# Writing a 64-expert loop out on all engines, moving the token lists behind gate-and-up, and dropping empty scatter entries

## The reference

```python
def moe(x, w_router, router_bias, w_gate_e, w_up_e, w_down_e, w_gate_s, w_up_s, w_down_s):
    t = x.reshape(-1, D_MODEL)
    ...
    def expert_step(acc, xs):
        wg, wu, wd, g = xs
        h = jax.nn.silu(t @ wg) * (t @ wu)
        return acc + (h @ wd) * g[:, None].astype(t.dtype), None
    routed, _ = lax.scan(expert_step, jnp.zeros_like(t), (w_gate_e, w_up_e, w_down_e, gates.T))
    shared = (jax.nn.silu(t @ w_gate_s) * (t @ w_up_s)) @ w_down_s
    return (routed + shared).reshape(shp)
```

## Time and profile before

| what | value |
|---|---|
| median of three runs | 1395.07 us |
| profiled execution, its own time: its span | 1394.2 us |
| PE busy | 1241.1 us (89%) |
| DVE busy | 777.2 us (56%) |
| ACT busy | 543.3 us (39%) |
| POOL busy | 407.7 us (29%) |
| DMA, mean over the span | 228 GB/s |
| loads of gate, up and down, each | 64 x 1024 KB |

### The profile page before, as it was taken

The page is one execution under the profiler, slowest core; times in us unless marked ns, Lnnn a source line. Parts: engine busy times, 40 slices in busy tenths (PEclk is TensorE's granted clock), DMA queues, the critical chain, the costliest instruction groups (busy, mean ns, idle before and its releaser), DMA issues.

```text
span 1394.2 us, 18458 instructions
## 1 busy us (share of the span) xinstructions
PE 1241.1 (89%) x6931; PEld 976.8 (70%) x6931; DVE 777.2 (56%) x1095; ACT 543.3 (39%) x722; POOL 407.7 (29%) x385
## 2 busy tenths in 40 slices
PE   6499978989999899969999999999999999999980
PEld 6499956789999897427666666666666666666650
DVE  2113589243311644537776666666666666666745
ACT  2231467242213312125444444444444444445522
POOL 2000234111100123251433343433444333433223
PEclk9699989599999997989999999999999999999995
DMA  9942020113223308327999999999999999999954
GB/s 191 286 151 81 16 86 2 68 38 100 76 91 115 126 1 343 147 83 276 365 361 350 343 345 343 346 340 342 351 347 342 344 334 341 342 343 342 356 106 152
DMA packets 92096, 317.49 MB, mean 228 GB/s; under 512 B 15586, under 2 KB 48516, under 8 KB 66804
## 3 DMA queue, kind: packets, MB, share of 16 engines
q1 hardware_dynamic: 65616, 257.03, 47.5%
q0 software_dynamic: 19280, 56.12, 20.5%
q10 hardware_dynamic: 7140, 3.50, 0.9%
HBM read 284.30 MB, written 47.97 MB: 238 GB/s over the span
## 4 chain that ended last, share of the span: by engine, by line
PE 77%; DVE 10%; issue 4%; DMA 3%; ACTq 2%; POOL 2%; ACT 2%; DVEq 0%; SPq 0%; POOLq 0%
PE bank L1925 26%; PE bank L1945 16%; PE bank L1661 9%; PE bank L1662 9%; PE bank L1820 4%; DVE onehot L1501 3%; PE bank L1888 3%; PE bank L1676 3%; ACTq L876 2%; PE bank L1850 2%; DVE L L1256 1%; DMA raw<-in_w_in_dram 1%; DVE mx L1262 1%; PE bank L1841 1%; PE bank L1867 1%
## 5 line engine op out<-in xcount | busy, mean ns | idle before, releaser
L1525 DVE TENSOR_TENSOR wgu_lo<-wgu,wgu_hi 128x4096 fp32r<-128x4096 f32 x64 | 282.5, 4414 | 2.7 <-ACT wgu_hi L1125 2.6
L788 POOL TENSOR_TENSOR spare<-spare 128x1 f32<-128x1 f32 x128 | 122.6, 958 | 445.7 <-DMA y_rows<-ysb,idx_u 406.1
L1945 PE MATMUL bank<-wd,hT 128*128 128x512 f32 x512 | 230.1, 592 | 0.9 <-DVE hT L1535 0.9
L1125 ACT ACTIVATE wgu_hi<-wgu 128x4096 fp32r<-128x4096 f32 x63 | 227.4, 3610 | 0.1
L1925 PE MATMUL bank<-wgu_hi,xgT 128*128 128x512 f32 x512 | 206.3, 403 | 2.6
L1925 PE MATMUL bank<-wgu_hi,xgT_lo 128*128 128x512 f32 x512 | 200.9, 392 | 0.0
L1925 PE MATMUL bank<-wgu_lo,xgT 128*128 128x512 f32 x512 | 200.6, 392 | 0.0
L1129 ACT ACTIVATE silu<-bank 128x256 f32<-128x256 f32 x64 | 24.5, 383 | 370.1 <-PE bank L1925 370.1
L1945 PEld LDWEIGHTS bank<-wd,hT 128*128 128x128 f32 x512 | 96.7, 189 | 98.0 <-issue 92.0
L1541 DVE COPY ysb<-bank 128x512 f32<-128x512 f32 x64 | 44.2, 691 | 162.5 <-PE bank L1945 162.5
L1925 PEld LDWEIGHTS bank<-wgu_hi,xgT 128*128 128x128 f32 x512 | 96.7, 189 | 23.4 <-issue 0.5
(11 more groups left out here) (287 smaller groups left out, 2391.6 us busy)
## 6 DMA issues: line engine op xcount, KB each, us to landing
wgu<-in_w_gate_e_dram SPq DMA_DIRECT2D x64, 1024.0 KB, 9.2
wgu<-in_w_up_e_dram SPq DMA_DIRECT2D x64, 1024.0 KB, 13.6
wd<-in_w_down_e_dram SPq DMA_DIRECT2D x64, 1024.0 KB, 7.8
raw<-in_w_in_dram SPq DMA_DIRECT2D x16, 1024.0 KB, 5.5
raw<-in_w_proj_a_dram SPq DMA_DIRECT2D x4, 1024.0 KB, 5.2
raw<-in_w_out_dram SPq DMA_DIRECT2D x4, 1024.0 KB, 5.2
bias_rows<-e_row POOLq DMA_DIRECT2D x1, 3072.0 KB, 34.6
x_lo_kept<-xT_lo SPq DMA_DIRECT2D x1, 2304.0 KB, 10.8
```

Of the source, the lines that this page charges most:

```text
L788: pool.tensor_tensor(spare[:, i:i + 1], spare[:, 0:1], spare[:, 0:1], ALU.mult).then_inc(s, 1)
L1125: act.activation(wgu_hi[u % 2][:], wgu[u % WSLOTS][:], ACT.Copy).then_inc(hi_by_act, 1)
L1525: v.tensor_tensor(wgu_lo[u % WSLOTS][:], w_[:], wgu_hi[u % 2][:].bitcast(F32), ALU.subtract).then_inc(lo_by_dve, 1)
L1945: last = mm(bank[3 + h][:, :], hT[:, u % 2, j, :], wd[slot][:, j, h * 512:(h + 1) * 512], start=j == 0, stop=j == FE // P - 1)
```

## The change

Three things.

1. The hardware loops of the experts are replaced, on SP, POOL, ACT, DVE and PE, by Python loops over all 64 experts. Every semaphore target and address is then a constant; there are no register instructions, branches or turns.
2. In PE's step `token_list(e + 4)` moves from ahead of `gate_up(e)` to behind it, ahead of `down(e - 1)`.
3. The scatter-add gets the same bounds check as the gather (row numbers over 575 are dropped). The 128 extra rows of `y_rows`, their zeroing on POOL and its semaphores go; one wait of ACT on the zeroing becomes a wait on the work ahead of it.

```diff
-    y_rows = nc.dram_tensor("y_rows", (TOK + P, D), F32, kind="Internal").ap()
+    y_rows = nc.dram_tensor("y_rows", (TOK, D), F32, kind="Internal").ap()
...
-            for e in range(WSLOTS, UNROLL):
-                load_expert(e, e, e - WSLOTS + 1)
-            with sp.Fori(1, E // UNROLL) as i:
-                for u in range(UNROLL):
-                    load_expert(i * UNROLL + u, u, i * UNROLL + (u - WSLOTS + 1))
+            for e in range(WSLOTS, E):
+                load_expert(e, e % UNROLL, e - WSLOTS + 1)
...
-            pool.wait_ge(pool_vs, NT)
-            pool.memset(sgln[:], 0.0).then_inc(pool_zero, 1)
-            pool.wait_ge(pool_zero, 1)
-            pool.dma_start(y_rows[TOK:TOK + P, :], sgln[:].rearrange("p a n -> p (a n)")).then_inc(y_zeroed, 16)
             for u in range(UA):
                 norm(u)
...
                 pool.indirect_dma_start(out=y_rows, out_offset=bass.IndirectOffsetOnAxis(idx_u[:, u:u + 1], 0),
-                                        in_=ysb[:, u % 2, :], in_offset=None, compute_op=ALU.add).then_inc(y_added, 16)
+                                        in_=ysb[:, u % 2, :], in_offset=None, compute_op=ALU.add,
+                                        bounds_check=bound, oob_is_err=False).then_inc(y_added, 16)
...
-            with pool.Fori(1, E // UNROLL - 1) as i:
-                for u in range(UNROLL):
-                    gather(i * UNROLL + (u + XGSLOTS), (u + XGSLOTS) % UNROLL)
-                    scatter(i * UNROLL + (u - 1), (u - 1) % UNROLL)
-            for e in range(E - UNROLL, E):
+            for e in range(E):
                 if e + XGSLOTS < E:
                     gather(e + XGSLOTS, (e + XGSLOTS) % UNROLL)
-                scatter(e - 1, (e - 1) % UNROLL)
-            scatter(E - 1, UNROLL - 1)
+                if e >= 1:
+                    scatter(e - 1, (e - 1) % UNROLL, e == 1)
+            scatter(E - 1, (E - 1) % UNROLL)
...
-            act.wait_ge(y_zeroed, 16)
+            act.wait_ge(pool_vs, NT)
...
                 if not last:
                     rows_t(e + 1, u + 1, (turn * (UNROLL // XGSLOTS) + ((u + 1) // XGSLOTS + 1)) * 16)
+                gate_up(e, u, wait=not first)
                 if ahead:
                     token_list(e + IDX_AHEAD, u + IDX_AHEAD)
-                gate_up(e, u, wait=not first)
                 if not first:
                     up = u - 1
                     down(e - 1, up, turn * (UNROLL // WSLOTS) + (up // WSLOTS + 1), wait=first is not None)
                 hidden_t(e, u)
 
-            for e in range(UNROLL):
-                step(e, e, 0, first=True if e == 0 else None if e == 1 else False)
-            with pe.Fori(1, E // UNROLL - 1) as i:
-                for u in range(UNROLL):
-                    step(i * UNROLL + u, u, i)
-            for e in range(E - UNROLL, E):
-                step(e, e % UNROLL, E // UNROLL - 1, ahead=e + IDX_AHEAD < E, last=e == E - 1)
+            for e in range(E):
+                step(e, e % UNROLL, e // UNROLL, first=True if e == 0 else None if e == 1 else False,
+                     ahead=e + IDX_AHEAD < E, last=e == E - 1)
```

More of the change, by code:

```diff
@@ L408, in hybrid_layer @@
     y_inited = sems("y_inited", 2)
-    y_zeroed = sem("y_zeroed")
     shared_landed = sem("shared_landed")
@@ L425, in hybrid_layer @@
     pool_scaled = sem("pool_scaled")
-    pool_zero = sem("pool_zero")
     pool_final = sem("pool_final")
@@ L828, in scatter @@
                 pool.indirect_dma_start(out=y_rows, out_offset=bass.IndirectOffsetOnAxis(idx_u[:, u:u + 1], 0),
-                                        in_=ysb[:, u % 2, :], in_offset=None, compute_op=ALU.add).then_inc(y_added, 16)
+                                        in_=ysb[:, u % 2, :], in_offset=None, compute_op=ALU.add,
+                                        bounds_check=bound, oob_is_err=False).then_inc(y_added, 16)
             pool.wait_ge(y_inited[0], 16 * ((NT + 1) // 2))
             pool.wait_ge(y_inited[1], 16 * (NT // 2))
-            pool.wait_ge(y_zeroed, 16)
-            for e in range(UNROLL):
-                gather(e + XGSLOTS, (e + XGSLOTS) % UNROLL)
-                if e >= 1:
-                    scatter(e - 1, e - 1, e == 1)
-            with pool.Fori(1, E // UNROLL - 1) as i:
-                for u in range(UNROLL):
-                    gather(i * UNROLL + (u + XGSLOTS), (u + XGSLOTS) % UNROLL)
-                    scatter(i * UNROLL + (u - 1), (u - 1) % UNROLL)
-            for e in range(E - UNROLL, E):
+            for e in range(E):
                 if e + XGSLOTS < E:
                     gather(e + XGSLOTS, (e + XGSLOTS) % UNROLL)
-                scatter(e - 1, (e - 1) % UNROLL)
-            scatter(E - 1, UNROLL - 1)
+                if e >= 1:
+                    scatter(e - 1, (e - 1) % UNROLL, e == 1)
+            scatter(E - 1, (E - 1) % UNROLL)
             pool.wait_ge(y_added, 16 * E)
@@ L864, in _ @@
                         pool.indirect_dma_start(out=y_rows, out_offset=bass.IndirectOffsetOnAxis(idx_u[:, 0:1], 0),
-                                                in_=ysb[:, 0, :], in_offset=None, compute_op=ALU.add).then_inc(y_added, 16)
+                                                in_=ysb[:, 0, :], in_offset=None, compute_op=ALU.add,
+                                                bounds_check=bound, oob_is_err=False).then_inc(y_added, 16)
                         pool.wait_ge(y_added, 16 * n + 16)
@@ L1154, in step @@
                     ex_y(e - 1, u - 1, free)
-            for e in range(UNROLL):
-                step(e, e, 0, first=e == 0, free=e >= 3)
-            with act.Fori(1, E // UNROLL - 1) as i:
-                for u in range(UNROLL):
-                    step(i * UNROLL + u, u, i)
-            for e in range(E - UNROLL, E):
-                step(e, e % UNROLL, E // UNROLL - 1, last=e == E - 1, ahead=e + 2 < E)
+            for e in range(E):
+                step(e, e % UNROLL, e // UNROLL, first=e == 0, last=e == E - 1, ahead=e + 2 < E, free=e >= 3)
             ex_y(E - 1, E - 1)
@@ L1573, in step @@
                     y_evac(e - 1, u - 1, free)
[L1575 to L1581, removed]
+            for e in range(E):
+                step(e, e % UNROLL, first=e == 0, ahead=e + IDX_AHEAD < E, wait=e + IDX_AHEAD >= UNROLL, last=e == E - 1,
+                     free=e >= 3)
             ht_evac(E - 1, E - 1)
```

## The result

| kernel | median us | lowest to highest | runs |
|---|---|---|---|
| before | 1396.01 | 1385.5 to 1398.42 | 9 |
| changed | 1403.04 | 1398.09 to 1405.88 | 9 |

The ratio is 1.006 (95% interval 1.0044 to 1.0077): the changed kernel is 7 us slower, less than the 1% that was called a difference ahead. The forecast was 1382, with a range of 1362 to 1398. The profiled execution of the changed kernel took 1398.09 us, its span 1396.4.

A forecast was written before the change was run, and what follows sets the result against it. Weight loads on the loaded DMA engines, 11.4 us per step, were to bind once PE needs 10.31; -9.3 in the loop, -2 behind the last load and -1 for scatter issues gave 1382 us, range 1362 to 1398.

The forecast's parts named there:

- weight loads at 11.4: Expert loop: unheld loads come every 11.05 to 11.45 us, taken 11.4, and set the step; -9.3 us; chance 0.77.
- Its rows on the loaded engines stay, so 0 for the loop.: Scatter-add with bounds check: real rows stay on the loaded DMA engines, so the check gains 0 in the loop.
- PE's step of 10.31: PE in the expert loop, written out with lists after gate-and-up: step falls from 11.61 to 10.31 us.
- The dropped rows lie on idle engines: Scatter-add's DMA: the check removes rows only from engines with least to do; main case with loads as bound, 0.77.
- Were the drop spread evenly: First rival: scatter takes 1.41 us, DMA step 9.96, PE's 10.31 binds; -65 us, some 1330; chance 0.13.
- The issue with a check takes a gather's 1.07: POOL: a scatter-add's issue with bounds check falls from 1.58 us to a gather's 1.07.
- the -1 for the last two issues: End of the kernel: two scatter-add issues on POOL, each 0.5 us shorter with the check, gain 1 us.
- The -2 behind the last load: Last load's landing to its gate-and-up: 13.1 us falls to 11, within 9.3 to 13.1; taken as -2 us.
- Zeroing, SP's loads, code blocks at nothing: Dropped zeroing on POOL, SP's unchanged waits and fetched instruction blocks cost or gain nothing; blocks slowing an engine: rival, 0.07.
- Gathers at nothing: Gathers are issued a fraction of a step later with three steps in hand, so no effect.
- What would show it: Profile signs: ACT waiting for loads in most steps, gate-and-up starts 11.3 to 11.5 apart, 40 to 60 more small packets.
- The sum: -9.3 - 2 - 1 = -12.3 on the profiled 1394.2 gives 1381.9; median lies 0.9 above; forecast 1382.

The follow-up runs named there:

- a_two_sums: The changed kernel with scatter-adds of even and odd experts going to two arrays, added at the end: 1387.6 us.
- b_spread_one: The changed kernel with list entries placed in other partitions, so that real rows spread over all DMA engines: 1322.24 us, ratio 0.9485 to the kernel before.
- a_two_sums_nc: The changed kernel with two scatter-add arrays and no bounds check on the scatter-add, empty entries going to extra zeroed rows: 1390.67 us.
- c_even_engines: The changed kernel with list entries permuted by a control table, the first 64 filling every second DMA engine with 8 rows: 1403.72 us.
- b_spread_nc: The changed kernel with list entries spread over the DMA engines but no bounds check on the scatter-add, all 128 rows added: 1371.31 us.

## Why the prediction was wrong

The failed step is the choice of the bound, weight loads at 11.4, and one sentence closed the way to the right one: "Its rows on the loaded engines stay, so 0 for the loop." I priced the scatter-add as load on the DMA engines and as an issue at the very end, and never as a chain of its own. Each one waits for the last to land, so issue, landing and POOL's fence make a period that no other engine can shorten.

The kernel before held the warning. There POOL's fence waited for a landing in each of the 46 steps from 726 to 1259 us, 6.6 us on average (first line; us in total, times, longest), while DVE's output copy waited for PE alone (second line):

```profile
POOL spare L788 <- DMA y_rows<-ysb,idx_u: 302.9, 46, 7.4
...
DVE ysb L1541 <- PE bank L1945: 117.7, 46, 2.6
```

The timeline of one step there:

```profile
800.14 1.58 POOL L828 DMA_INDIRECT y_rows<-ysb,idx_u  x1 [0.15 <-issue]
...
807.14 4.42 DVE L1525 TENSOR_TENSOR wgu_lo<-wgu,wgu_hi 128x4096 fp32r<-128x4096 f32 x1
...
809.14 2.47 POOL L788 TENSOR_TENSOR spare<-spare 128x1 f32<-128x1 f32 x1 [5.98 <-DMA y_rows<-ysb,idx_u]
...
811.77 1.58 POOL L828 DMA_INDIRECT y_rows<-ysb,idx_u  x1 [0.15 <-issue]
```

From issue to issue is 11.63 us, PE's step, but only because DVE's low parts hold the fence until 811.6. With a fence of 0.18 us, 9.5 us to landing and the 0.8 to 0.9 us that POOL then takes are 10.3 to 10.4 (an estimate), some 1.2 us under PE's 11.61. That is already no less than the 10.31 that I wanted of PE. A rival was missing: the scatter-add's chain as the bound.

Its size: the landing takes 11.0 us where it took 9.5, and the parts do not simply add up. A third output buffer takes 0.6 off (10.4), so that much goes with the meeting with DVE. The check is worth 0.7 in the old loop, 0.2 in the written-out one. What is left has no experiment of its own. With 0.8 to 0.9 on POOL the period is 11.8 to 11.9 (11.87 measured). In the 47 steps in which ACT waited for a landing, 0.4 to 0.5 above the loads' 11.4 make 19 to 22 us, so 1401 to 1404 by my own sum, where 1403 was measured. The other way round, a_two_sums without the 6.9 us of its end is at 1381 (an estimate): with that chain out of the way, the forecast of 1382 comes out, though not each of its terms (below).

- *PE's step of 10.31*: right. 10.26 in b_spread_one, and list matmuls of 0.28 us without a wait.
- *A load's step of 11.4*: right in size (11.33 in a_two_sums), but not the bound. In the changed kernel ACT waits for loads in 15 steps; after 880 us it waits for none, since the scatter-add's chain is slower.
- *The dropped rows lie on idle engines*: right (a_two_sums against a_two_sums_nc, c_even_engines against b_spread_one). "Were the drop spread evenly", which I costed at a step below PE's 10.31 and some 1330, is what b_spread_one does, at 1322.
- *The issue with a check takes a gather's 1.07*: wrong. It is 1.58 with or without the check, and 2.07 where it meets DVE's one-hot, so the -1 for the last two issues was not there to gain. The -2 behind the last load has no run of its own.
- *Zeroing, SP's loads, code blocks at nothing*: nothing in the runs speaks against it. *Gathers at nothing*: the gather's fence is held up by DVE, but its issue is over before the next landing.
- *What would show it*: ACT waiting in most steps and starts 11.3 to 11.5 apart did not come; the 48 small packets did.
- *The sum*: 1381.9 and the 0.9 added to it make 1382.8, not 1382; nothing hangs on it.

## What to carry to other kernels

For each serial chain (a transfer that waits for its own predecessor) write down its period from issue to next issue, and compare it with the step that you mean to reach, not with the step of today. A shorter step also brings together instructions that today run apart: look at what one landing releases on all engines. Where a list leaves part of 128 partitions empty, ask on which DMA engines the real rows lie: spreading them was worth 5%, and only together with the faster PE step.

## What the runs showed of the hardware beyond that

In the old loop, dropping 56 of 128 rows by a bounds check made the scatter-add land later, not sooner (10.2 against 9.5 us); written out it was 11.0 against 10.8, and with two accumulators it landed sooner. With the rows spread over the engines, the drop brought the landing from 10.2 us to 7.5 (b_spread_nc, b_spread_one). The issue on POOL takes the same 1.58 us with and without a check, though a gather's takes 1.05. An issue that starts while DVE runs an instruction on two SBUF tiles is held for what is left of it, less some 0.1 us: 0.49 us by the one-hot, up to 4.2 by the low parts.
